# Key scores of the dilation-16 group moved out of the retention stage of a hybrid decoder step

## The chip, the cores and the metric

One core of a Trainium2 chip. The metric is the device time of one launch in microseconds (us), median of the runs. Before the change it is 1073.62 us over 3 runs (1072.58 to 1073.82).

## The reference

One step of a one-layer decoder for a prompt of 512 tokens and for 8 sample batches of 8 tokens, all in float32 (each product is made of three matmuls over high and low parts). A projection of x (1024 columns) to 10240 columns feeds two branches:

- A: attention with 4 head slots of 128 and three groups (window, dilation) = (128, 1), (512, 4), (2048, 16). A query reads the keys at distances 0, d, 2d, ..., window, with a penalty that grows with the distance. The sample queries read theirs from the caches of the 8 batches.
- B: retention with 4 heads (key 128, value 256), a carried state per batch, and a norm per head.

Both are gated, projected, merged, projected again and normalised. The caches are outputs too: every cache row from the eighth on is copied to the output, 8 rows further ahead, and the new keys and values are put behind.

For dilation 16 and cached keys, what concerns us is

```python
for b, q, h, m:   # 8 batches, 8 queries, 4 head slots, 128 keys
    s[b, q, h, m] = dot(query[b, q, h], cache2048[b, 16 * m + q, 0, h]) * scale - slope * (2048 - 16 * m)
```

Query q of a batch reads only the cache rows 16m + q: no two queries share a key.

## The kernel before

Instructions of five engines are written out by hand and tied by semaphores; every engine works through its own list in order. SyncE (SP) issues nearly all DMAs, on one queue. The stages:

**Attention stage** (span 24 to 409 us, a loop over 4 head slots of about 96 us). A head slot consumes six weight chunks of 1 MB. SP issues a chunk's two halves (`columns`, line 385) as soon as the half of `raw` is free, that is when its previous content has been split: ScalarE makes the high part (`high`, line 1132), VectorE the low part (`low`, line 1368) and increments `w_low`. Between chunks SP issues the copies of the caches of five batches (`rows`, line 417, DRAM to DRAM: 2.09 MB for each batch and head slot of the largest cache). TensorE projects in 27 units of about 3 us (`natural`, `transposed`) into two alternating banks, which VectorE empties (`unit_free`), and does the prompt's attention between the units. Unit 5 is the first of the second chunk, unit 10 the first of the third, unit 14 of the fourth, unit 18 of the fifth, unit 23 of the sixth. ScalarE's order (`attention_head`) ends with: `probs(1, 6)`, `next_high(5)` (the high part of the next head slot's first chunk), `sigmoid(23)`, `probs(2, 8)`, and so on; VectorE's `zr(0)` waits for `sigmoid(23)`, and TensorE's `output(1)` for VectorE's `output(0)` behind it. GpSimd stores keys and values (`store_kv`).

**Retention stage** (409 to 812 us, a loop over 4 retention heads of about 98 us, each with two sample batches x = 0, 1). For each batch SP loads 13 key tiles and then 13 value tiles of 128 x 512 (tile 0: dilation 1, tiles 1 to 4: dilation 4, tiles 5 to 12: dilation 16) into three slots (`load_tiles`, `keys`, `values`). A key tile is transposed by TensorE (4 transposes, line 680), split by ScalarE and VectorE (lines 1256 and 1574), and multiplied with block matrices of the queries (`score_tile`, 8 matmuls, line 919). `rows(x)` on VectorE collects the scores, then come softmax, the probabilities (`cached_probs`, `probs`) and the value tiles (`cached_output`, line 958). Units of the retention's own projections stand between. The low parts of the two weight chunks of the next head are made by GpSimd (lines 632 and 641). `vown`, 8 rows of 2 KB in each of three loads, are the batch's own values (line 479).

**Last stage** (812 to 1071 us): gates, branch projections, the copies of the caches of the other three batches, the output projection and the norm.

## Time and profile before

| | before |
|---|---|
| median of 3 runs | 1073.62 us |
| profiled execution: its own time, its span | 1073.26 us, 1071.40 us |
| TensorE matmul busy | 999.7 us (93%), mean granted clock 0.974 |
| VectorE, ScalarE, GpSimd busy | 539.9, 380.3, 151.2 us |
| DMA moved | 219.5 MB, mean 205 GB/s |
| attention stage, DMA share by halves of a head slot | 0.75 and 0.54 |
| retention stage from 440 us on, GB/s over stretches of 35 to 62 us | 153 to 211 |

The span is the time from the first to the last instruction on the core; the own time of the execution is 1.86 us longer. Busy times are summed over instructions, and matmuls overlap: a group's mean duration is longer than the time that the next one has to wait.

### The profile page before, as it was taken

The page shows a single profiled execution, that of the slowest core. Times are in us where ns is not written, and L with a number is a line of the kernel's source. Part 1 is how long each engine was busy: PE and PEld are TensorE (multiplying, and loading weights), DVE is VectorE, ACT ScalarE, POOL GpSimd, SP SyncE. Part 2 cuts the span into 40 slices and gives each one's busy share as a digit, 9 for nine tenths or more (in the row PEclk, how much of TensorE's full clock was granted, in tenths as well). Part 3 has the DMA queues.
Part 4 walks back from the last instruction along what each step waited for, and adds up shares of the span by engine and source line. Part 5 has one row for each costly group of instructions (what it writes and reads, how often), then busy time and mean ns, then how long its engine had stood idle before and what let it go on. Part 6 is the DMA issues. An engine that isn't in the chain of part 4 may idle for free.

```text
span 1071.4 us, 21575 instructions
## 1 busy us (share of the span) xinstructions
PE 999.7 (93%) x7796; PEld 926.7 (86%) x7796; DVE 539.9 (50%) x1017; ACT 380.3 (35%) x605; POOL 151.2 (14%) x149
## 2 busy tenths in 40 slices
PE   5999999999999999999989989999988999999892
PEld 5999999999999999778877777878757999999892
DVE  4246335433633454566656755675675433224338
ACT  4035213422431344345425442633454334333100
POOL 0001010101101012232312231322210000000003
PEclk8999999999999999999999999999988999999997
DMA  8775674767556564365638454643680888776602
GB/s 284 247 258 192 229 255 168 255 234 260 184 198 208 206 229 168 130 227 207 203 109 277 154 184 141 243 167 130 207 281 20 281 286 297 256 264 232 216 21 88
DMA packets 137317, 219.51 MB, mean 205 GB/s; under 512 B 7936, under 2 KB 102784, under 8 KB 135552
## 3 DMA queue, kind: packets, MB, share of 16 engines
q1 hardware_dynamic: 132704, 205.77, 56.5%
q0 software_dynamic: 3920, 10.89, 3.0%
q10 hardware_dynamic: 656, 2.36, 0.6%
q8 instruction: 23, 0.38, 0.2%
q14 instruction: 14, 0.11, 0.0%
HBM read 206.40 MB, written 99.88 MB: 286 GB/s over the span
## 4 chain that ended last, share of the span: by engine, by line
PE 84%; DVE 9%; ACT 3%; issue 2%; DMA 1%; DVEq 0%; ACTq 0%; SPq 0%; POOL 0%; POOLq 0%
PE bank L685 18%; PE bank L687 18%; PE bank L686 18%; PE bank L680 8%; PE bank L715 4%; PE bank L958 4%; PE bank L919 3%; DVE part_l L1574 3%; PE bank L772 2%; PE bank L794 2%; PE bank L994 1%; PE bank L1003 1%; PE bank L936 1%; ACT part_h L1256 1%; DMA xn<-in_x_prompt_dram 1%
## 5 line engine op out<-in xcount | busy, mean ns | idle before, releaser
L685 PE MATMUL bank<-xh,wh 128*128 128x288 f32 x640 | 193.1, 302 | 0.4 <-PE bank L1091 0.4
L685 PE MATMUL bank<-wh,xh 128*128 128x256 f32 x640 | 188.1, 294 | 3.5 <-DVE wl L1368 3.0
L687 PE MATMUL bank<-xh,wl 128*128 128x288 f32 x640 | 189.3, 296 | 0.0
L686 PE MATMUL bank<-xl,wh 128*128 128x288 f32 x640 | 189.2, 296 | 0.0
L686 PE MATMUL bank<-wl,xh 128*128 128x256 f32 x640 | 183.2, 286 | 0.0
L687 PE MATMUL bank<-wh,xl 128*128 128x256 f32 x640 | 183.1, 286 | 0.0
L685 PEld LDWEIGHTS bank<-wh,xh 128*128 128x128 f32 x640 | 125.3, 196 | 6.3 <-issue 3.4
L1132 ACT ACTIVATE wh<-raw 128x1024 fp32r<-128x1024 f32 (+1 forms) x104 | 101.2, 1018 | 80.1 <-PE bank L715 69.8
L686 PEld LDWEIGHTS bank<-wl,xh 128*128 128x128 f32 x640 | 125.2, 196 | 1.4
L687 PEld LDWEIGHTS bank<-wh,xl 128*128 128x128 f32 x640 | 124.8, 195 | 0.0
L685 PEld LDWEIGHTS bank<-xh,wh 128*128 128x128 f32 x640 | 121.0, 189 | 1.7 <-issue 1.4
L686 PEld LDWEIGHTS bank<-xl,wh 128*128 128x128 f32 x640 | 120.9, 189 | 1.0 <-issue 1.0
L1368 DVE TENSOR_TENSOR wl<-raw,wh 128x1024 fp32r<-128x1024 f32 (+1 forms) x90 | 102.3, 1173 | 36.8 <-ACT wh L1132 26.7
L687 PEld LDWEIGHTS bank<-xh,wl 128*128 128x128 f32 x640 | 120.8, 189 | 0.0
L1273 ACT ACTIVATE part_h<-cslot 128x512 fp32r<-128x512 f32 x104 | 59.4, 621 | 102.1 <-PE bank L958 101.6
L1574 DVE TENSOR_TENSOR part_l<-bank,part_h 128x512 fp32r<-128x512 f32 x104 | 71.1, 690 | 29.4 <-ACT part_h L1256 28.9
L1256 ACT ACTIVATE part_h<-bank 128x512 fp32r<-128x512 f32 x104 | 61.3, 597 | 49.7 <-PE bank L680 49.6
L1574 DVE TENSOR_TENSOR part_l<-cslot,part_h 128x512 fp32r<-128x512 f32 x104 | 66.6, 684 | 17.6 <-ACT part_h L1273 17.3
L919 PE MATMUL bank<-part_h,qm 128*64 128x128 f32 x416 | 68.5, 242 | 2.1 <-DVE part_l L1574 2.1
L577 POOL DMA_DIRECT2D out_dram<-kv x24 | 17.0, 710 | 353.0 <-DVE vn L1428 353.0
L680 PE MATMUL bank<-con,cslot 128*128 128x128 f32 x416 | 64.7, 281 | 2.0 <-DVE part_l L1574 1.5
L919 PE MATMUL bank<-part_l,qm 128*64 128x128 f32 x416 | 60.6, 222 | 0.0
(208 smaller groups left out, 1844.6 us busy)
## 6 DMA issues: line engine op xcount, KB each, us to landing
cslot<-in_cache_kv_w_dram SPq DMA_DIRECT2D x48, 1024.0 KB, 5.9
out_dram<-in_cache_kv_w_dram SPq DMA_DIRECT2D x20, 2040.0 KB, 10.4
raw<-in_w_in_dram SPq DMA_DIRECT2D x128, 256.0 KB
out_dram<-in_cache_kv_w_dram SPq DMA_DIRECT2D x24, 1020.0 KB, 9.5
out_dram<-in_cache_kv_w_dram SPq DMA_DIRECT2D x20, 504.0 KB, 5.2
raw<-in_w_in_dram SPq DMA_DIRECT2D x16, 512.0 KB
out_dram<-in_cache_kv_w_dram SPq DMA_DIRECT2D x24, 252.0 KB, 3.2
out_dram<-kv POOLq DMA_DIRECT2D x16, 256.0 KB, 3.3
```

What stands on the lines that cost most here:

```text
L680: return pe.transpose(out, in_, ident[0:k, 0:k])
L685: pe.matmul(out, lhs[0](k), rhs[0](k), start=(k == 0), stop=False)
L686: pe.matmul(out, lhs[0](k), rhs[1](k), start=False, stop=False)
L687: last = pe.matmul(out, lhs[1](k), rhs[0](k), start=False, stop=(k == n - 1))
L715: last = pe.matmul(out, pair[:, k, 0:P], part(k), start=(k == 0 and n == 0), stop=(k == KT_N - 1 and n == 1))
L919: last = pe.matmul(bank[4][0:BLK, g * P:(g + 1) * P], qm[:, o:o + BLK], part[j % 3][:, h * P:(h + 1) * P], start=(m == 0 and h == 0 and i ...
L958: last = pe.matmul(bank[4][0:BLK, :], probs, part[i % 3][0:n, :], start=(i == 0 and part is part_h), stop=(i == TILES and part is part_l))
L1132: act.activation(wh[par][:, s * HW:s * HW + n], wraw[s][:, 0:n], ACT.Copy).then_inc(w_high, 1)
L1256: act.activation(part_h[j % 3][:, :], bank[2 + j % 2][:, :], ACT.Copy).then_inc(part_high, 1)
L1273: act.activation(part_h[i % 3][:, :], cslot[s][:, k, :], ACT.Copy).then_inc(part_high, 1)
L1368: tt(wl[par][:, s * HW:s * HW + n], wraw[s][:, 0:n], wh[par][:, s * HW:s * HW + n].bitcast(F32), ALU.subtract).then_inc(w_low, 1)
L1574: tt(part_l[i % 3][:, :], src[:, :], part_h[i % 3][:, :].bitcast(F32), ALU.subtract)\
```

## The change

It has two parts.

1. The cached keys of dilation 16 (tiles 5 to 12 of the key tiles) are no longer loaded, transposed, split and multiplied in the retention stage; `KTILES` is 5. Instead, in each head slot h of the attention stage, SP loads these keys by query (`far_keys`): a partition holds one (half of m, batch, query), and 64 keys of 128 numbers, in three parts of 24, 24 and 16 keys into two buffers `far`. A part is 16 DMAs of 8 partitions each. GpSimd multiplies 8 keys at a time with the query's row (`qrow`; TensorE turns the queries `qdup`, ScalarE copies them out), and VectorE sums each product (`far_sum`, 8 per head slot, named among its other work). The sums go through DRAM (`fscr`) into `fars`, where `rows(x)` of the retention stage adds the penalty. `far_keys(h, 2)` waits for `far_sum(2)` of the same head slot and stands ahead of the sixth weight chunk; `far_keys(h, 0)` waits for the last sum of the head slot before.
2. The copies of the fifth batch's caches leave the attention stage and are issued in the retention stage, between that stage's loads. The low parts of the retention stage's weight chunks go from GpSimd to VectorE, at places of their own, and its order of units is changed: `value_unit(1)`, `value_unit(2)` and `cached_probs(0)` directly after `cached_scores(0)`, and the state groups inside `cached_output(0)`. Values of slots 1 and 2 of a head's first batch are loaded with the keys.

The core of the diff (semaphores, counts, and the reordering of ScalarE's and VectorE's lists that follows from it are left out):

```diff
-TILES = 13
+KTILES, TILES = 5, 13
 VTILES = TILES + 1
-PARTS = TILES + VTILES
+PARTS = KTILES + VTILES
...
+FAR = ((0, 24), (24, 48), (48, 64))
+FAR_PIECE = 8
+FAR_PIECES = 64 // FAR_PIECE
...
+            def far_keys(h, c):
+
+                lo, hi = FAR[c]
+                sp.wait_ge(far_summed, h * FAR_PIECES + (FAR_PIECES, 6, FAR_PIECES + 3)[c])
+                settle(sp)
+                src = caches[2].rearrange("b (m q) c h e -> b q m c (h e)", q=16)
+                for mh in range(2):
+                    for b in range(DEC_B):
+                        p = mh * 64 + b * DEC_T
+                        sp.dma_start(far[c % 2][p:p + DEC_T, 0:hi - lo, :],
+                                     src[b, 0:DEC_T, mh * 64 + lo:mh * 64 + hi, 0, bass.ds(h * DH, DH)])\
+                            .then_inc(far_in[c], 16)
...
                     columns(h * A_CH + (j + 1), (h * DH + a, h * DH + b), DH)
+                    if j < 2:
+                        far_keys(h, j)
                     rows(2, j, h * 510, 510)
                 columns(h * A_CH + 5, (h * RV + OFF_ZR,), CW)
-                rows(2, 4, h * 510, 510)
+                far_keys(h, 2)
...
-                for b in range(A_COPY_B):
+                for b in range(A_COPY_B - 1):
...
-                values(r * 2)
-                keys(r * 2 + 1, (0,))
+                values(r * 2, (0,))
+                keys(r * 2 + 1)
                 sp.wait_ge(states_out, r + 2)
                 if last:
                     gate_chunk(C0_C, 0)
                 else:
                     settle(sp)
                     retention_chunk(r * B_CH + (C0_B + 2), r + 1, 0)
-                keys(r * 2 + 1, (1, 2))
+                rows(2, A_COPY_B - 1, r * 510, 255)
+                values(r * 2 + 1)
                 if not last:
                     retention_chunk(r * B_CH + (C0_B + 3), r + 1, 1)
-                values(r * 2 + 1)
+                rows(2, A_COPY_B - 1, r * 510 + 255, 255)
+                rows(1, A_COPY_B - 1, r * 126, 126)
+                rows(0, A_COPY_B - 1, r * 30, 30)
                 if not last:
                     sp.wait_ge(rt_free[1], r * 9 + 6)
                     settle(sp)
                     head_constants(r + 1)
                     keys(r * 2 + 2)
+                    values(r * 2 + 2, (1, 2))
...
+                pool.wait_ge(far_row, h + 1)
+                for c, (lo, hi) in enumerate(FAR):
+                    pool.wait_ge(far_in[c], h * 256 + 256)
+                    for m in range(0, hi - lo, FAR_PIECE):
+                        a = far[c % 2][:, m:m + FAR_PIECE, :]
+                        tt(a, a, qrow[:, :].rearrange("p (a e) -> p a e", a=1).to_broadcast([P, FAR_PIECE, DH]),
+                           ALU.mult).then_inc(far_prod, 1)
                 pool.wait_ge(unit_free, h * A_UNITS + (3 + 23))
                 store_kv(h, 1)
+                pool.wait_ge(far_summed, h * FAR_PIECES + 2 * FAR_PIECES)
+                settle(pool)
+                pool.dma_start(fscr[bass.ds(h, 1), :, :].rearrange("h p m -> p (h m)"), fsum[:, :]).then_inc(far_out, 16)
+                pool.wait_ge(far_out, h * 16 + 16)
+                pool.sem_inc(far_free, 1)
...
+            for h in range(H):
+                pool.dma_start(fars[64 + h * DEC_T:64 + (h + 1) * DEC_T, :].rearrange("q (x m) -> q x m", m=64),
+                               fscr[h].rearrange("(x q) m -> q x m", q=DEC_T)).then_inc(far_back, 16)
...
-                for s in range(2):
-                    pool.wait_ge(w_high, r * (2 * B_CH) + (2 * C0_B + 4 + s + 1))
-                    tt(wl[0][:, s * HW:(s + 1) * HW], wraw[s], wh[0][:, s * HW:(s + 1) * HW].bitcast(F32),
-                       ALU.subtract).then_inc(w_low, 1)
...
+                    if u == 15:
+                        pe.wait_ge(unit_free, h * A_UNITS + (3 + 15))
+                        pe.wait_ge(o_read, h * QBLK + 1)
+                        turn(bank[2][:, P:2 * P], qdup[:, :]).then_inc(far_turned, 1)
...
+                act.wait_ge(far_summed, h * FAR_PIECES + FAR_PIECES)
+                act.wait_ge(far_turned, h + 1)
+                act.activation(qrow[:, :], bank[2][:, P:2 * P], ACT.Copy).then_inc(far_row, 1)
...
+                    dve.tensor_reduce(fsum[:, n * FAR_PIECE:(n + 1) * FAR_PIECE], far[c % 2][:, m:m + FAR_PIECE, :],
+                                      AX.X, ALU.add).then_inc(far_summed, 1)
...
                 values(18)
+                far_sum(0)
                 values(19)
                 low(c + 5, 1)
+                far_sum(1)
                 values(20)
                 softmax(2)
+                far_sum(2)
                 values(21)
                 probs(1, 5)
+                far_sum(3)
                 values(22)
                 softmax(3)
+                far_sum(4)
                 zr(0)
                 output(0)
                 probs(2, 7)
                 output(1)
+                far_sum(5)
                 low(c + 6, 0)
                 zr(1)
                 probs(3, 9)
+                far_sum(6)
                 output(2)
                 probs(3, 11)
                 zr(2)
+                far_sum(7)
                 output(3)
                 zr(3)
...
+                    o = fars[64:64 + ROWS, :].rearrange("p (a b m) -> p a b m", a=2, m=64)
+                    tt(srow[:, 2 * P:3 * P].rearrange("p (a m) -> p a m", a=2),
+                       o[:, :, bass.ds(r * 2 + x, 1), :].rearrange("p a b m -> p a (b m)"),
+                       const("biasc", ROWS)[:, 2 * P:3 * P].rearrange("p (a m) -> p a m", a=2), ALU.add)
...
-                lows(1, 0, 4, TILES)
+                lows(1, 0, 4, KTILES)
                 rows(1)
+                low(C0_C if last else r * B_CH + (C0_B + 2), 0)
                 normalise_rows(1)
...
-                lows(1, 1, 7, 11)
+                lows(1, 1, 7, 9)
+                if not last:
+                    low(r * B_CH + (C0_B + 3), 1)
+                lows(1, 1, 9, 11)
```

## Rows read from the trace of the kernel before

**Rows 1.** The profile's page: the chain that ended last, by engine

```profile
PE 84%; DVE 9%; ACT 3%; issue 2%; DMA 1%; DVEq 0%; ACTq 0%; SPq 0%; POOL 0%; POOLq 0%
```

**Rows 2.** A stretch: length, busy PE, PEld, DVE, ACT, POOL; clock, DMA share, GB/s

```profile
264.00:312.00 48.00, 47.66 (x366) 45.67 (x365) 23.98 (x45) 19.13 (x27) 3.88 (x6) 1.00 0.54 193
```

**Rows 3.** Timeline of TensorE and VectorE, second retention head: start, us, line

```profile
523.80 0.30 PE L919 MATMUL bank<-part_h,qm 128*64 128x128 f32 x1
...
536.53 1.56 PE L936 MATMUL bank<-ktn,qm 128*64 x24
...
578.19 1.28 DVE L1574 TENSOR_TENSOR part_l<-bank,part_h 128x512 fp32r<-128x512 f32 x2
...
586.53 0.69 DVE L1574 TENSOR_TENSOR part_l<-bank,part_h 128x512 fp32r<-128x512 f32 x1 [0.25 <-ACT part_h L1256]
```

**Rows 4.** Groups by line: score matmuls, and subtractions on VectorE and GpSimd

```profile
L1368 DVE TENSOR_TENSOR wl<-raw,wh 128x1024 fp32r<-128x1024 f32 (+1 forms) x90 | 102.3, 1173 | 36.8 <-ACT wh L1132 26.7 <-DMA lnb<-in_ln_b_dram 10.0
...
L919 PE MATMUL bank<-part_h,qm 128*64 128x128 f32 x416 | 68.5, 242 | 2.1 <-DVE part_l L1574 2.1
...
L632 POOL TENSOR_TENSOR wl<-raw,wh 128x1024 fp32r<-128x1024 f32 x8 | 18.9, 2375 | 61.3 <-ACT wh L1132 61.3
```

**Rows 5.** Timeline of VectorE, third attention head

```profile
231.53 0.43 DVE L1416 COPY kv<-bank 128x256 f32<-128x256 f32 x1
233.81 0.42 DVE L1416 COPY kv<-bank 128x256 f32<-128x256 f32 x1 [1.85 <-PE bank L687]
...
248.95 0.45 DVE L1403 TENSOR_SCALAR qt<-bank 128x288 f32<-128x288 f32 x1
...
283.04 1.22 DVE L1446 TENSOR_REDUCE nmax<-scoresp 128x1 f32<-128x1024 f32 x1
...
305.47 0.46 DVE L1408 TENSOR_TENSOR yb<-bank,sg 128x288 f32 x1 [3.24 <-ACT sg L1155]
```

**Rows 6.** Timeline of ScalarE, same head

```profile
286.81 2.00 ACT L1132 ACTIVATE wh<-raw 128x1024 fp32r<-128x1024 f32 x2 [1.01 <-PE bank L715]
288.83 1.28 ACT L1155 ACT_TABLE_LOAD   x1
292.13 0.41 ACT L1155 ACTIVATE sg<-bank 128x288 f32<-128x288 f32 x1 [2.01 <-PE bank L687]
```

**Rows 7.** Timeline of SyncE's DMA queue, same head

```profile
218.54 2.23 SPq L385 DMA_DIRECT2D raw<-in_w_in_dram  x4
...
258.56 1.54 SPq L385 DMA_DIRECT2D raw<-in_w_in_dram  x2
...
278.26 2.21 SPq L385 DMA_DIRECT2D raw<-in_w_in_dram  x4
```

**Rows 8.** DMA issues: a narrow load, and a wide one's landing

```profile
L479 SPq DMA_DIRECT2D vown<-out_dram x24: 277/294/578, 429.5 to 778.9; - x24
...
cslot<-in_cache_kv_w_dram SPq DMA_DIRECT2D x16, 256.0 KB, 2.9
```

**Rows 9.** Stretches: weight load, cache copy, loads of z (two), loads of vown

```profile
221.00:222.00 1.00, 1.00 (x11) 1.00 (x10) 0.00 (x0) 0.00 (x0) 0.00 (x0) 1.00 0.98 293
...
226.00:227.00 1.00, 1.00 (x10) 1.00 (x10) 0.42 (x1) 0.00 (x0) 0.00 (x0) 1.00 0.86 326
...
1000.00:1001.00 1.00, 1.00 (x6) 1.00 (x6) 0.00 (x0) 0.00 (x0) 0.00 (x0) 0.50 1.02 418
...
1002.00:1003.00 1.00, 1.00 (x11) 1.00 (x10) 0.00 (x0) 0.00 (x0) 0.00 (x0) 1.00 1.06 193
...
533.20:533.40 0.20, 0.20 (x5) 0.20 (x3) 0.20 (x1) 0.00 (x0) 0.00 (x0) 1.00 0.59 72
533.40:533.60 0.20, 0.20 (x6) 0.20 (x5) 0.20 (x1) 0.02 (x1) 0.00 (x0) 1.00 0.37 92
```

**Rows 10.** Stretches with the granted clock, end of the retention stage

```profile
812.00:814.00 2.00, 1.65 (x7) 1.56 (x8) 0.00 (x0) 1.50 (x1) 0.00 (x0) 0.50 0.00 0
...
816.00:818.00 2.00, 2.00 (x15) 2.00 (x14) 1.32 (x1) 2.00 (x1) 0.00 (x0) 0.82 0.00 0
```

More of the change, by code:

```diff
@@ L249, in bass_hybrid_step @@
         rinv = sb("rinv", [P, QBLK], F32, scope_a)
+        far = [sb(f"far{b}", [P, 24, DH], F32, scope_a) for b in range(2)]
+        qdup = sb("qdup", [P, P], F32, scope_a)
+        qrow = sb("qrow", [P, DH], F32, scope_a)
+        fsum = sb("fsum", [P, 64], F32, scope_a)
+        fscr = nc.dram_tensor("fscr", (H, P, 64), F32, kind="Internal").ap()
         scope_a.close()
@@ L473, in values @@
                     tiles = SLOTS[slot]
-                    load_tiles(b, 1, slot, tiles, PARTS + tiles[1])
+                    load_tiles(b, 1, slot, tiles, (PARTS if slot == 0 else KTILES) + tiles[1])
                     if slot == 0:
@@ L1712, in retention_head @@
                 values(0)
-                lows(0, 0, 2, TILES)
+                lows(0, 0, 2, KTILES)
+                rows(0)
+                values(1)
+                normalise_rows(0)
+                lows(0, 1, 0, 3)
+                values(2)
+                probs(0)
                 dve.wait_ge(hcon_in, r * 16 + 16)
@@ L1761, in retention_head @@
                 next_projected(2)
[L1762 removed]
+                lows(1, 1, 7, 9)
+                if not last:
+                    low(r * B_CH + (C0_B + 3), 1)
+                lows(1, 1, 9, 11)
                 normalise()
```

143 lines of the change are left out of this document (70 added, 73 removed).

## The prediction

> **What bounds the kernel now.** I read the chain of waits first: 84% of it is TensorE [rows 1]. Then the stretches: in the second half of a head slot of the attention stage TensorE is busy 47.66 of 48 us, VectorE half of that time, GpSimd 3.88 us [rows 2]. So nearly every microsecond of TensorE work taken away shortens the kernel, and every stall of TensorE lengthens it. The DMA share of 0.54 there looks like room. But a share is a mean; what counts is which load stands ahead of the one that TensorE needs next.
>
> **What the change takes away.** The score matmuls are listed with 242 ns each [rows 4], and 8 of them for each of 64 key tiles would be 124 us. That is wrong, as they overlap. The timeline gives the real price: in the second retention head the 13 key tiles of x = 0 run from 523.80 to 536.53 [rows 3], 0.98 us each, so 8 tiles are 7.8 us. In x = 1 VectorE splits tiles 4 and 5 from 578.19 on and tile 12 until 587.2 [rows 3]; tiles 5 to 12 are 8.3 us. Together 16.1 us a head, 64 us in all.
>
> **What the retention stage gives back.** GpSimd's two pairs of subtractions, 2.375 us a piece, go to VectorE, which needs 1.17 us for one [rows 4]. In x = 1 the first pair now stands after `rows(1)`: TensorE has about 2.9 us of output groups to do after the last score, VectorE 2.3 us of `rows` and 2.4 us of lows, so the next projection starts some 1.8 us late. The second pair falls into the value tiles, where VectorE has little spare time: 1.2 us. I take 3 us for three heads and 1.5 us for the last, 10 us; the bounds are 0 and 17 (all of VectorE's new time on the path). For x = 0 I followed the new order through: the probabilities come out under units 1 and 2, and the stalls are as long as before. Its DMAs sum to about 16 MB a head, against 18 MB now, and come between waits that leave them time; the copies of the fifth batch cost nothing here as long as the values of x = 1 (3.4 MB, issued when its fifth key tile is split) land within the some 16 us until TensorE's sixth value tile. **Retention: -54 us.** At the hand-over GpSimd's four small DMAs and their landing stand ahead of `a_end` and of VectorE's first work: +2 us.
>
> **What the attention stage pays.** GpSimd's 8 products (up to 2.4 us each, as its subtractions of the same size, rows 4) and VectorE's 8 sums (1.22 us each, as the maximum over 1024 numbers, rows 5) a head slot lie beside TensorE work; both engines are idle half the time or more. 2 us in all for what sticks out, with the 4 turns. The price is in the loads.
>
> *The wait in SP's queue.* Now SP issues the sixth chunk's successor at 278.26 [rows 7], and ScalarE takes it at 286.81, then loads a table and does `sigmoid(23)` at 292.13 [rows 6]; VectorE's `zr(0)` and `output(0)` follow within 2 us and release TensorE. With the change `far_keys(h, 2)` stands ahead of it and waits for `far_sum(2)`, after the reduction of 283.04: 284.26 + 1.22 = 285.5. SP has stood there since the two DMAs at 258.56 [rows 7]. Then come 16 narrow issues: 0.294 us each for one of 8 partitions [rows 8], with address work about 0.5 us, 8.0 us in all. Queued behind this wait are four weight DMAs and eight copies; behind the weights wait ScalarE's whole list, VectorE's `zr(0)`, TensorE's `output(1)`. The stall can't be less than that of the issues alone.
>
> *How fast narrow loads run* the trace shows only in part. A weight load moves 293 GB/s, a cache copy 326 [rows 9]. The load of `z` goes at 418 GB/s over 128 partitions and at 193 over 64, at the same DMA share [rows 9]: the rate goes with the partitions. The three 8-partition loads of `vown` pass in slices of 72 and 92 GB/s [rows 9]. So the bounds are 82 (their mean) and 293 GB/s. I take 130: above the nearest row, as its 48 KB hold a start and an end, and a train of 16 can overlap. The Trainium skill (DMA: Bandwidth & Descriptors, "How many engines (k)") says that a DMA uses as many engines as divide the slowest dimension of both sides, 8 here, which would be half of 293, or 147 GB/s, and a result of 1089 us by the working below.
>
> *The sum for a head slot, at 130 GB/s.* Parts 0 and 1 are 1.57 MB (12.1 us), part 2 is 1.05 MB (8.1 us). A wide 256 KB load lands 2.9 us after its issue [rows 8], of which 0.9 is transfer: 2.0 us on top of a queue's transfers.
> - Part 2: 285.5 + 8.1 + 3.6 (the weights at 293 GB/s) + 2.0 = 299.2; ScalarE's second half 1.0, the table 1.3: `sigmoid(23)` at 301.5 instead of 292.13, **9.4 us**. TensorE's granted clock is 0.50 in the 4 us after it starts again at 812, and 0.82 in the next 2 [rows 10]: full speed comes back about 5 us late, **2 us** more.
> - Part 0 is issued when the last sum is done, after the product at 305.47: 307.1, or 211.1 on the clock of the head slot shown (96 us earlier). Its 12.1 us, the copy behind it (2.09 MB, 6.4 us) and the weights (3.6 + 2.0) end at 235.2; ScalarE and VectorE need 2.2 us for them and 0.4 for the copy of unit 5, now at 231.53, which may end at 233.8, where the next unit's copy starts [rows 5]: 237.8, **4.0 us**. Now these weights, issued at 218.54 [rows 7], find an empty queue.
> - Part 1 goes out behind them, from 234.5: 12.1 + 6.4 + 3.6 + 0.7 + 2.6 = 259.9, where VectorE's 248.95 [rows 5] may slip to 252, now 256: **3.9 us**.
>
> 19.3 us a head slot, 77 us in all. Moving the fifth batch's copy away helps none of the three, since it stood behind the fifth chunk.
>
> **Sum,** against the profiled execution's own 1073.26 (0.4 under the median): -54 + 2 + 2 + 77 = +27, **1100 us**.
>
> **The rivals.**
> - *Narrow loads run as wide ones.* At 293 GB/s parts 0 and 1 are out of the way in time and only the wait of part 2 stays, by its issues: 11.5 us a head slot with the clock, 46 us: 1069 us; with nothing given back in the retention stage 1059. For it speaks that no narrow train is in the trace; against it the row of 193 GB/s. It decides from about 12 us lost a head slot: below, the change is faster. Chance 0.24.
> - *Narrow loads run at 82 GB/s.* Part 0 takes 19.2 us, part 2 12.8 us. Stalls: 14.1 + 2, 11.1 and 11.0 us, 38 us a head slot: 1176 us. For it speak the rows of `vown`; against it that a load may overtake the stuck one. Chance 0.17. The Trainium skill (SBUF — State Buffer, "Door 1: The DMA port swizzle") gives each 4 neighbouring partitions one port of about 27 GB/s, so 8 partitions 54 GB/s, which would make about 1280 us; the rows of 193 and 72 GB/s go its way.
> - *VectorE becomes the bound in the retention stage* (17 us given back instead of 10): 1107 us, the same side; it only widens.
>
> **How the numbers follow.** The forecast's case has 0.53, the first rival 0.24, the second 0.17; 0.06 is for an outcome near the old time. The forecast's case spans 1080 (147 GB/s and less given back) to 1130 (105 GB/s). The range of 1055 to 1150 adds the first rival whole; it leaves out most of the second. 0.2% (2.1 us) is about what a measurement tells from no change: faster 0.25, same 0.05, slower 0.70.
>
> **What the profile after would show.** Right: score matmuls 160 instead of 416 of each kind; retention heads of about 84 us instead of 98; in each head slot a TensorE gap of about 9 us before `output(1)` that ends with ScalarE behind a DMA of weights, and gaps of 3 to 5 us at units 7 and 13; head slots of 115 us instead of 96; a DMA share near half during the narrow loads. Wrong: weights that land in time behind parts 0 and 1, or a gap at `output(1)` under 7 us (issues under 0.4 us); a gap over 12 us would be the slow rival; retention heads over 88 us would say that VectorE or the values' loads bind there.

## The result and the profile after

The changed kernel takes 1176.95 us (median of 4 runs, 1172.77 to 1196.41) beside 1073.72 us for the kernel before on the same chip: ratio 1.094, 95% interval 1.090 to 1.099. Ratios, here and below, leave out the executions that took over 1.5% longer than the fastest of the same kernel, here the one of 1196.41 us. The forecast was 1100 us with a range to 1150; the prediction had the side right and the size wrong, by 77 us. The second rival had named 1176 us.

The profiled execution took 1172.77 us (span 1171.1). First the chain of waits, by engine; before, TensorE had 84% of it and SP's queue nothing [rows 1]:

```profile
PE 54%; SPq 15%; issue 8%; DVE 8%; DMA 8%; POOL 3%; ACT 2%; DVEq 0%; POOLq 0%; ACTq 0%
```

Of the chain, 23% now belong to SP's queue and to DMAs; the question is in which stage. Two instructions mark the stages: VectorE's low half of the sample queries, the first thing it does after the attention stage, and the last of the eight `pn` matmuls, near the end of the retention stage. A row gives count, shortest/median/longest ns, and the first and last start. Before:

```profile
L1529 DVE TENSOR_TENSOR qhl<-qhl x1: 959/959/959, 412.0 to 412.0; 128x768 fp32r<-128x768 f32 x1
L958 PE MATMUL bank<-part_h,pn x8: 443/446/681, 472.6 to 806.5; 24*64 24x512 f32 x8
```

After:

```profile
L1583 DVE TENSOR_TENSOR qhl<-qhl x1: 959/959/959, 580.1 to 580.1; 128x768 fp32r<-128x768 f32 x1
L999 PE MATMUL bank<-part_h,pn x8: 443/447/681, 629.8 to 906.4; 24*64 24x512 f32 x8
```

So the attention stage is 168 us longer (580.1 - 412.0). From there to the end of the span it was 659.4 us and is 591.0: **68 us shorter**, of which 57 lie between the first and the last `pn` matmul (333.9 and 276.6 us). 168 - 68 = 100 us, the difference of the spans. From marker to end, a stretch (columns as in [rows 2]) and waits of TensorE that changed (total, times, longest), before:

```profile
412.00:1071.40 659.40, 601.23 (x4721) 538.26 (x4719) 359.72 (x689) 252.99 (x440) 118.17 (x93) 0.96 0.57 194
PE bank L958 <- DVE part_l L1574: 13.3, 17, 3.2
PE bank L680 <- DVE qdt L1730: 8.4, 4, 2.1
```

After:

```profile
580.10:1171.10 591.00, 536.31 (x3948) 476.93 (x3947) 332.12 (x647) 209.66 (x349) 84.14 (x79) 0.96 0.60 207
PE bank L999 <- DVE part_l L1628: 9.3, 12, 3.2
PE bank L722 <- DVE wl L1399: 5.1, 4, 1.5
```

So 65 of the 68 us are TensorE work that is gone (601.23 - 536.31), and 3.5 are idle time that is gone. The score matmuls are 160 of each kind instead of 416 [rows 4]:

```profile
L960 PE MATMUL bank<-part_h,qm 128*64 128x128 f32 x160 | 25.5, 241 | 4.8 <-DVE part_l L1628 4.8
...
L621 POOL TENSOR_TENSOR far<-far,qrow 128x1024 f32<-128x1024 f32 x32 | 75.3, 2382 | 190.9 <-DMA far<-in_cache_kv_w_dram 113.4 <-ACT qrow L1226 77.5
...
L1532 DVE TENSOR_REDUCE fsum<-far 128x8 f32<-128x1024 f32 x32 | 38.7, 1210 | 0.9 <-DVE yb L1443 0.9
```

The new work costs what its nearest rows said (2.38 and 1.21 us each); but GpSimd stood 113 us in front of its loads, over the four head slots.

Where the attention stage lost its time shows in one head slot, 246 to 386 us. What TensorE waited for there (total, times, longest):

```profile
PE bank L834 <- DVE on L1495: 18.7, 1, 18.7
PE bank L722 <- DVE kv L1451: 16.7, 1, 16.7
PE bank L722 <- DVE qt L1438: 7.7, 1, 7.7
```

Three gaps, 43 us, in the three places that the prediction had named: `output(1)`, unit 7, unit 13. The first two come in all four head slots (13 to 19.5 us each); the third, at unit 13, is 7.7 us here, 2.3 us in the slot before, and missing in the first and the last. The same slot in stretches (columns as in [rows 2]), and three stretches inside narrow trains (a train is the row of transfers that makes up one part):

```profile
256.00:266.00 10.00, 0.52 (x5) 0.28 (x3) 0.39 (x1) 0.00 (x0) 0.00 (x0) 0.72 1.01 94
266.00:276.00 10.00, 0.79 (x3) 0.79 (x4) 1.64 (x5) 5.99 (x7) 7.72 (x7) 0.50 1.08 306
...
316.00:326.00 10.00, 0.00 (x0) 0.00 (x0) 0.00 (x0) 0.08 (x1) 0.00 (x0) 0.62 0.83 208
326.00:336.00 10.00, 5.19 (x26) 5.19 (x27) 3.21 (x4) 2.03 (x2) 0.00 (x0) 0.52 0.64 92
...
252.00:254.00 2.00, 2.00 (x17) 2.00 (x16) 1.97 (x4) 0.00 (x0) 0.00 (x0) 1.00 0.65 67
302.00:304.00 2.00, 2.00 (x19) 2.00 (x19) 0.41 (x1) 0.00 (x0) 0.00 (x0) 1.00 0.65 59
338.00:340.00 2.00, 2.00 (x19) 2.00 (x18) 0.42 (x1) 0.00 (x0) 0.00 (x0) 1.00 0.65 88
```

During part 2 (252 to 254) the queue moves 67 GB/s, during part 0 (302 to 304) 59, and 88 in part 1, where 130 had been assumed; a weight load moves 293 [rows 9]. The DMA share of 0.65 does not warn of it: the engines show as busy while they move little. The granted clock is 0.50 to 0.72 over the stretches with the gaps, so a gap costs a little more than its length. SP's queue in the same slot (start, us):

```profile
221.33 1.56 SPq L396 DMA_DIRECT2D raw<-in_w_in_dram  x2
248.55 8.45 SPq L440 DMA_DIRECT2D far<-in_cache_kv_w_dram  x16
257.36 7.46 SPq L396 DMA_DIRECT2D raw<-in_w_in_dram  x4
265.11 8.29 SPq L428 DMA_DIRECT2D out_dram<-in_cache_kv_w_dram  x8
281.12 2.23 SPq L396 DMA_DIRECT2D raw<-in_w_in_dram  x4
```

SP stands from 222.9 to 248.55 before it can issue part 2, and four weight DMAs come behind it at 257.36. These are the first chunk of the next head slot. The sixth chunk is the pair at 221.33: what the section on the change says of part 2, that it stands ahead of the sixth chunk, is one chunk off. It stands behind the sixth and ahead of the next head slot's first, as the prediction's working has it ("the sixth chunk's successor").

### The profile page after: what moved, and what is told of

The parts are those of the page before. It is cut to its first block, busy times and chain, and to the rows that moved or that the text cites. A ratio compares the mean times of both kernels' runs of the same rounds, so it can differ in the third digit from the quotient of the medians.

```text
span 1171.1 us, 20225 instructions
## 1 busy us (share of the span) xinstructions
PE 958.4 (82%) x7032; PEld 887.2 (76%) x7032; DVE 548.4 (47%) x1011; ACT 340.2 (29%) x518; POOL 197.0 (17%) x175
## 4 chain that ended last, share of the span: by engine, by line
PE 54%; SPq 15%; issue 8%; DVE 8%; DMA 8%; POOL 3%; ACT 2%; DVEq 0%; POOLq 0%; ACTq 0%
PE bank L722 13%; PE bank L723 12%; PE bank L724 12%; SPq L440 10%; DMA raw<-in_w_in_dram 7%; SPq L396 5%; PE bank L999 4%; PE bank L717 3%; PE bank L752 2%; PE bank L834 2%; DVE part_l L1628 1%; PE bank L1044 1%; PE bank L809 1%; PE bank L1035 1%; DMA xn<-in_x_prompt_dram 1%
## 5 line engine op out<-in xcount | busy, mean ns | idle before, releaser
L722 PE MATMUL bank<-wh,xh 128*128 128x256 f32 x640 | 192.5, 301 | 67.9 <-DVE kv L1451 59.2
L722 PE MATMUL bank<-xh,wh 128*128 128x288 f32 x640 | 197.6, 309 | 10.4 <-DVE qt L1438 10.0
L723 PE MATMUL bank<-wl,xh 128*128 128x256 f32 x640 | 187.3, 293 | 0.0
L1399 DVE TENSOR_TENSOR wl<-raw,wh 128x1024 fp32r<-128x1024 f32 (+1 forms) x104 | 120.0, 1184 | 121.9 <-ACT wh L1173 107.7
L722 PEld LDWEIGHTS bank<-xh,wh 128*128 128x128 f32 x640 | 124.8, 195 | 12.1 <-DVE qt L1438 10.5
L724 PEld LDWEIGHTS bank<-wh,xl 128*128 128x128 f32 x640 | 129.2, 202 | 0.0
L621 POOL TENSOR_TENSOR far<-far,qrow 128x1024 f32<-128x1024 f32 x32 | 75.3, 2382 | 190.9 <-DMA far<-in_cache_kv_w_dram 113.4
L834 PE MATMUL bank<-kv,pt 128*128 128x128 f32 x216 | 32.4, 310 | 75.2 <-DVE on L1495 75.2
L834 PEld LDWEIGHTS bank<-kv,pt 128*128 128x128 f32 x216 | 30.4, 222 | 76.2 <-DVE on L1495 76.2
L1862 DVE TENSOR_TENSOR uc<-bank,sgc 128x288 f32<-128x288 f32 x32 | 14.6, 457 | 92.7 <-PE bank L724 92.7
L1443 DVE TENSOR_TENSOR yb<-bank,sg 128x288 f32 x16 | 7.3, 457 | 98.6 <-ACT sg L1196 98.6
```

Source lines behind the costliest of these rows:

```text
L621: tt(a, a, qrow[:, :].rearrange("p (a e) -> p a e", a=1).to_broadcast([P, FAR_PIECE, DH]), ALU.mult).then_inc(far_prod, 1)
L722: pe.matmul(out, lhs[0](k), rhs[0](k), start=(k == 0), stop=False)
L723: pe.matmul(out, lhs[0](k), rhs[1](k), start=False, stop=False)
L724: last = pe.matmul(out, lhs[1](k), rhs[0](k), start=False, stop=(k == n - 1))
L834: last = pe.matmul(bank[2][:, 0:P], pt[:, bi % 2, x * P:(x + 1) * P], kv[:, k, (G + g) * DH:(G + g + 1) * DH], start=(x == 0), stop=(x == ...
L1399: tt(wl[par][:, s * HW:s * HW + n], wraw[s][:, 0:n], wh[par][:, s * HW:s * HW + n].bitcast(F32), ALU.subtract).then_inc(w_low, 1)
```

## The experiments

Every time below is the median of its own runs; the kernel before had medians of 1073.7 to 1075.6 us beside them. "Marker" is the start of the instruction on `qhl` shown above, in the profiled execution: the end of the attention stage. A profiled execution can lie off the median: mostly by less than 5 us, in two kernels by 7, but the first series with the copies first was profiled at 1191.8 us, the second at 1143.8, and the strided kernel from GpSimd's queue, issued later, at 1077.8.

| kernel | us | marker, us |
|---|---|---|
| before / after | 1073.7 / 1177.0 | 412.0 / 580.1 |
| 16 neighbouring partitions | 1101.7 | 506.5 |
| 8 partitions, 4 apart | 1138.6 | 544.6 |
| 16 partitions, 8 apart ("strided") | 1063.2 | 468.2 |
| strided, third part last | 1026.8 | 431.8 |
| narrow, third part last | 1074.9 | 476.6 |
| narrow, only SP's wait in the old place | 1125.1 | 531.8 |
| strided, only SP's wait in the old place | 1039.6 | 448.7 |
| no dilation-16 work at all | 1005.2 | 413.8 |
| strided last, thin products and sums | 1016.3 | 425.0 |
| strided last, fifth batch back | 1029.3 | 439.6 |
| strided last, parts 0 and 1 a chunk later | 1027.5 | 436.4 |
| strided last, copies first | 1025.2 | 434.7 |
| narrow, copies first, two series | 1158.2, 1153.7 | 599.2, 551.2 |
| narrow / strided from GpSimd's queue | 1147.9 / 1065.4 | 557.0 / 479.9 |
| the same, issued later | 1085.9 / 1068.2 | 489.6 / 485.9 |

**1. Is it the rate, and what sets it?** The kernel issues each part as 16 transfers, one for each batch and half, of 8 neighbouring partitions (the 8 query positions). Three other ways to move the same 512-byte pieces to the same buffers:

```
# e_neighbours: one transfer for each query position q, rows in the order (q, batch, half)
-   sp.dma_start(far[c % 2][p:p + DEC_T, 0:hi - lo, :], src[b, 0:DEC_T, ...])      # 16 times
+   sp.dma_start(far[c % 2][q * 16:q * 16 + 16, 0:hi - lo, :], src[:, q, lo:hi, ...])  # 8 times
# e_strided: rows in the order (batch, half, q)
+   sp.dma_start(far[c % 2][q:q + 15 * DEC_T + 1:DEC_T, 0:hi - lo, :], src[:, q, lo:hi, ...])
# e_spread: 16 transfers, p = j // 4 * 32 + j % 4
+   sp.dma_start(far[c % 2][p:p + 4 * DEC_T - 3:4, 0:hi - lo, :], src[j // 2, 0:DEC_T, ...])
```

The first two reorder the queries and the sums to fit.

> The same bytes to the same buffers, but a part comes as 8 transfers of 16 neighbouring partitions (one query position q each) in place of 16 transfers of 8 neighbouring ones. Theory P (what limits the narrow loads is how many write ports of SBUF their few neighbouring partitions reach; partitions that lie far apart would go faster): 16 neighbours reach at most twice as many as 8, so the part runs at 60 to 120 GB/s instead of the 59 to 67 measured, and the time falls only partly, to 1080 to 1177 us. Theory E (a transfer of 8 partitions occupies only 8 of the 16 DMA engines, and where the partitions lie does not matter): 16 partitions occupy all 16 engines, so the rate is that of the strided layout of the next run, and the two times are the same. Theory S (the read side in DRAM, 512-byte pieces 64 KB apart, sets the rate): no change, 1170 to 1180 us.

> As the run before (8 transfers of 16 partitions, the same DRAM pieces in each), but the 16 partitions lie 8 apart and so are spread over the whole of SBUF. Theory P: the rate rises towards that of the wide loads (200 to 293 GB/s), and the time is 1030 to 1060 us, well under the run with 16 neighbours. Theory E: the same time as with 16 neighbours, whichever it is. Theory S: 1170 to 1180 us as the changed kernel.

> Still 16 transfers of 8 partitions a part, but the 8 partitions lie 4 apart instead of side by side. The query columns are not reordered, so the dilation-16 scores are of wrong queries; the work and its times are the same. Theory P: 8 partitions 4 apart reach four times the ports of 8 side by side; the rate doubles at least, to 120 GB/s or more, and the time is 1050 to 1120 us. Theory E: 8 engines at the same rate each, no change, 1170 to 1180 us. Theory S: no change either.

Measured: 1101.7 us (ratio to before 1.022, interval 1.018 to 1.027), 1063.2 (0.988, 0.985 to 0.991), 1138.6 (1.060, 1.055 to 1.064). Stretches inside the trains, first 16 neighbours, then 16 strided, then 8 spread:

```profile
230.00:232.00 2.00, 2.00 (x18) 2.00 (x17) 1.97 (x2) 0.00 (x0) 0.00 (x0) 1.00 1.24 118
268.00:270.00 2.00, 1.32 (x11) 1.12 (x10) 1.86 (x4) 0.00 (x0) 0.00 (x0) 1.00 1.28 112
```

```profile
214.00:216.00 2.00, 2.00 (x18) 2.00 (x17) 1.97 (x3) 0.00 (x0) 0.00 (x0) 1.00 0.56 148
250.00:252.00 2.00, 2.00 (x19) 2.00 (x18) 1.60 (x3) 0.00 (x0) 0.00 (x0) 1.00 1.21 188
```

```profile
290.00:292.00 2.00, 2.00 (x19) 2.00 (x19) 1.30 (x3) 1.73 (x2) 0.00 (x0) 1.00 0.40 110
292.00:294.00 2.00, 2.00 (x19) 2.00 (x18) 1.50 (x3) 0.00 (x0) 0.00 (x0) 1.00 0.41 123
```

The read side is the same in all, so DRAM is not what limits (theory S falls). Neighbours against strided: same number of transfers, same partitions in each, same pieces, only the distance differs, and 38 us come off; theory E alone falls, P stands. 8 neighbours against 8 spread, at a higher price to issue (0.70 us each instead of 0.43): 38 us again. The share points the same way: in these rows neighbours move 59 GB/s at a share of 0.65 or 118 at 1.24, some 90 to 95 per unit of engine time; spread moves 110 at 0.40, 275 per unit, up to three times as much. It is no fixed price of a layout: strided moves 264 per unit in the first of its rows and 155 in the second, and the last heading shows narrow trains of 154 GB/s at a share of 0.61. But P is not all: doubling the neighbours from 8 to 16 doubled the rate, and the spread train is held by its issues (16 in 14.4 us, 98 KB each, 109 GB/s). The Trainium skill (SBUF — State Buffer, "Door 1: The DMA port swizzle") gives every 4 neighbouring partitions one port of about 27 GB/s, with 32 partitions apart on the same port again. By that rule 8 neighbours get 54, 16 neighbours 108, and 16 partitions 8 apart only 8 ports, 216 GB/s; the rows have 59, 112 to 118, and 148 to 188. The trace agrees with its order and nearly with its sizes here; the narrow trains of a higher rate under the last heading, 104 to 154 GB/s with 8 neighbours, lie far above its 54.

**2. Where the third part stands.** `far_keys(h, 2)` is moved behind the weights that stood behind it, the next head slot's first chunk (in the last head slot the retention stage's first). The expectations call this "behind the sixth chunk's columns", one chunk off:

```
     columns(h * A_CH + 5, (h * RV + OFF_ZR,), CW)
-    far_keys(h, 2)
     if last: ... else: columns(h * A_CH + 6, ...)
+    far_keys(h, 2)
```

> The strided loads, and the third part of a head's dilation-16 keys is issued behind the sixth chunk's columns instead of ahead of them (in the last head it stays ahead of the retention stage's first columns, since both branches of the issue list put it right behind or ahead). Theory P with order: the wait of SP for the second part's sums no longer holds back the weights of the next head, so a further 3 to 7 us per head for three heads come off against the strided run: 1012 to 1040 us, under the kernel before. If the order does not matter: within 3 us of the strided run.

> The changed kernel with its narrow loads, the third part of a head's keys issued behind the sixth chunk's columns, in all four heads. Theory R (the rate of the narrow loads is the loss, since all three parts of 26, 26 and 17 us pass through one queue ahead of weights): some of the wait only moves to the next head's second chunk, so 5 to 30 us come off, 1145 to 1172 us. Theory O (the loss is mostly SP's wait for the second part's sums with weights queued behind it): the same 36 us come off as between the two strided runs, or more, so 1141 us or less.

(The first of these expectations is unsure of the last head; in both kernels the third part is last in all four.) Measured: strided 1026.8 us (ratio 0.955, 0.952 to 0.959), **under the kernel before**; narrow 1074.9 (0.997, 0.993 to 1.001; single runs from 1061 to 1086). Theory O wins clearly for the narrow loads: one line moved takes 102 us off, against 36 with the strided ones. That moved SP's wait for the sums together with the transfers. Then only the transfers were moved, and SP's wait for the sums left where it was:

```
-    far_keys(h, 2)
+    sp.wait_ge(far_summed, h * FAR_PIECES + (FAR_PIECES + 3))
     if last: ... else: columns(h * A_CH + 6, ...)
+    far_keys(h, 2)
```

> The changed kernel with only the transfers of the third part behind the sixth chunk's columns; SP's wait for this head's first three sums stays ahead of them. Moving wait and transfers together took 102 us off (1177 to 1075). Theory W (it is the wait: the sixth chunk's columns cannot be issued until VectorE has made its third sum, which itself waits for the late first part): most of the 102 us is back, 1140 to 1177 us. Theory T (it is the 17 us that the narrow transfers themselves take ahead of the columns): within 15 us of 1075 us.

> The same with the strided loads, between 1063 us (wait and transfers ahead) and 1027 us (both behind). Theory W: 1050 to 1063 us. Theory T: 1027 to 1037 us.

Measured: 1125.1 us (interval of the ratio 1.036 to 1.049) and 1039.6 (0.964 to 0.970). Neither theory has it alone: with narrow loads the transfers out of the way take 52 us off and the wait moved too another 50; with strided ones 24 and 13. What TensorE waited for, over the whole kernel, in the changed one:

```profile
PE bank L834 <- DVE on L1495: 75.2, 4, 19.5
PE bank L722 <- DVE kv L1451: 59.2, 5, 16.7
```

with the wait alone in the old place:

```profile
PE bank L724 <- DVE kv L1453: 57.7, 5, 16.8
PE bank L724 <- DVE qt L1440: 21.7, 3, 10.8
PE bank L836 <- DVE on L1497: 12.7, 4, 3.7
```

and with both moved:

```profile
PE bank L722 <- DVE kv L1451: 28.4, 7, 12.2
PE bank L834 <- DVE on L1495: 10.4, 8, 2.3
```

The transfers ahead of the weights made the gap at `output(1)` (75 us down to 13; the waits for `qt` rose from 10 to 22). The gap at unit 7 (`kv`) stayed until the wait moved too. But then the same transfers also ran faster, as told under the last heading. Part 0 of the third head slot, with the wait in the old place:

```profile
272.00:274.00 2.00, 2.00 (x19) 2.00 (x18) 1.21 (x3) 1.91 (x3) 0.00 (x0) 1.00 0.65 77
```

and with both moved:

```profile
252.00:254.00 2.00, 2.00 (x19) 2.00 (x18) 0.00 (x0) 0.05 (x1) 0.00 (x0) 1.00 0.62 111
```

So the 50 us hold two things, the wait and a faster part 0, and how they share them is not shown; the strided pair has 13 us for its wait.

**3. The rest of the change alone.** All dilation-16 work is left out (those cached scores are then zero before the bias), with the waits for it on TensorE and ScalarE; the retention stage and the copies stay as changed.

```
-    far_keys(h, j) ... far_keys(h, 2)                     # SP, all three parts
-    tt(a, a, qrow...)  ...  far_sum(0) ... far_sum(7)     # products and sums
-    turn(bank[2][:, P:2 * P], qdup[:, :]) ... act.activation(qrow[:, :], ...)
-    pool.dma_start(fscr...) ... pool.dma_start(fars[...], fscr[h]...)
+    pool.memset(fars[64:64 + ROWS, :], 0.0).then_inc(far_back, 16 * H)
```

> The changed kernel without the dilation-16 loads, products, sums and the detour of the queries: the dilation-16 scores of the cached keys are left out (zero before the bias), everything else of the change stays, the fifth batch's copies in the retention stage too. Theory of the prediction: the retention part of the change is worth 54 us net, so 1015 to 1022 us. Theory from the changed kernel's trace (the give-back of 10 us by the low halves on VectorE did not come): the time from the end of the attention stage on is 66 us shorter, so 1005 to 1012 us. Rival: the retention heads are short only because the late attention stage left the copies less to contend with; then over 1025 us.

Measured: 1005.2 us (ratio 0.933, 0.928 to 0.938), with the marker and a stretch:

```profile
L1544 DVE TENSOR_TENSOR qhl<-qhl x1: 957/957/957, 413.8 to 413.8; 128x768 fp32r<-128x768 f32 x1
```

```profile
100.00:200.00 100.00, 99.33 (x778) 96.87 (x777) 46.12 (x85) 30.53 (x41) 9.62 (x15) 1.00 0.58 194
```

The attention stage is as long as before (413.8 against 412.0): with TensorE busy 99.33 of 100 us, moving the fifth batch's copies out has nothing to gain there. The whole 69 us are the retention stage's, as in the changed kernel; the rival, that they come from a late attention stage, falls. That leaves a floor: a version with free dilation-16 work would take 1005 us, and the strided one with the third part last pays 22 us over it.

**4. What those 22 us are.** Products and sums on 8 of 128 elements, the scores then of 8 elements only:

```
-    a = far[c % 2][:, m:m + FAR_PIECE, :]
+    a = far[c % 2][:, m:m + FAR_PIECE, 0:8]     # and the same in qrow and in the sum
```

> The strided version with the third part last, but products and sums work on 8 of the 128 elements only (the dilation-16 scores are of 8 elements): all loads, waits and instruction counts stay, 19 us of GpSimd and 10 us of VectorE a head go to about a quarter. Theory L (what is left of the loss against the version without the dilation-16 work is loads in the queue ahead of weights): within 5 us of the 1026.8 us measured with whole products. Theory V (it is VectorE's sums that delay the low halves and evictions in order behind them): 8 us or more come off, 1008 to 1018 us.

Measured: 1016.3 us. 10.5 us are engine time of products and sums (theory V); the other 11 are the loads with what the thin products and sums still take, not taken apart. Over 200 to 300 us TensorE is busy 98.69 of 100, against 96.61 with whole ones. How much of the 10.5 is VectorE's and how much GpSimd's was not tried. The fifth batch's copies put back into the attention stage:

```
     columns(h * A_CH + 5, (h * RV + OFF_ZR,), CW)
+    rows(2, 4, h * 510, 510)
-    for b in range(A_COPY_B - 1):
+    for b in range(A_COPY_B):
...
-    rows(2, A_COPY_B - 1, ...) ... rows(0, A_COPY_B - 1, ...)     # stage_b
```

> The strided version with the third part last, and the fifth batch's copies (20 MB of traffic read and written) back in the attention stage as before the change. Theory Q (moving them made room in the attention stage's queue, which the new loads need): 10 to 25 us slower than 1026.8 us. Rival (they fit in either stage): within 3 us. Second rival: the retention stage gains more than the attention stage loses, 1015 to 1023 us.

Measured: 1029.3 us (1028.0 to 1031.8), against 1026.8 (1024.7 to 1031.2): the marker is 7.8 us later and what follows is 2.2 us shorter in the profiled executions, and the medians differ by 2.5 us, within the rival's 3. Moving the copies does next to nothing. Parts 0 and 1 a chunk later in the queue:

```
-    if j < 2:
-        far_keys(h, j)
+    if j in (1, 2):
+        far_keys(h, j - 1)
```

> The strided version with the third part last (1026.8 us), and the first and second part each one chunk later in SP's queue (behind the second and third chunk's columns). If only the third part's wait and place mattered: within 3 us. If each part costs by the chunk that stands behind it: the first head gains about 4 us at its start, where TensorE was idle for 4.2 of 36 us (24 to 60 us) that the version without dilation-16 work keeps busy, the others nothing: 1020 to 1026 us. If the products then come late for the sums: over 1030 us.

Measured: 1027.5 us (1019.7 to 1033.3), within the 3 us of the first expectation. The first head gains at its start and gives it back at once; stretches with parts 0 and 1 early, then late:

```profile
24.00:60.00 36.00, 31.80 (x240) 31.60 (x240) 8.76 (x18) 3.18 (x3) 1.58 (x3) 0.90 1.12 295
60.00:100.00 40.00, 40.00 (x306) 39.02 (x305) 22.32 (x38) 13.22 (x19) 16.53 (x10) 1.00 0.53 174
```

```profile
24.00:60.00 36.00, 36.00 (x290) 36.00 (x289) 12.66 (x23) 5.55 (x6) 3.93 (x6) 0.98 1.04 282
60.00:100.00 40.00, 36.24 (x257) 35.03 (x256) 18.25 (x32) 10.95 (x16) 14.09 (x6) 0.91 0.54 179
```

**5. The same loads from another queue.** `far_keys` is called by GpSimd instead of SP, so that no weight stands behind a narrow transfer in a queue.

```
 with pool.Fori(0, H) as h:
+    far_keys(h, 0)                                  # pool.dma_start in it
+    far_keys(h, 1)
     pool.wait_ge(unit_free, h * A_UNITS + (3 + 10))
...
                ALU.mult).then_inc(far_prod, 1)
+            if c == 1 and m == 0:
+                far_keys(h, 2)
```

> The changed kernel's narrow loads, the same transfers, but issued from GpSimd's queue (the first two parts of a head at the start of its turn, the third after the first product of the second part), so that no weight stands behind them in a queue. Theory Q (what costs is that weights stand behind slow transfers in one queue): 1015 to 1045 us, whatever the rate of the narrow loads. Theory B (narrow loads take the DMA engines' time itself, so weights are late from any queue): 1060 us or more. A third cost would be GpSimd's own time to issue 48 transfers a head.

> The same with the strided loads, 24 transfers a head from GpSimd's queue. Theory Q: about 10 to 15 us under the strided version with the third part last, 1010 to 1020 us, near the 1016 us of thin products; the rest to the 1005 us without dilation-16 work is VectorE's sums. Theory B: 1027 us or more, as there.

Measured: 1147.9 and 1065.4 us, on theory B's side. Both were clouded: the first parts ran against the kernel's first loads (TensorE waited 28.7 and 27.2 us for its first input `xn`, 10 us in the kernels of experiment 2), and GpSimd itself waited 13.8 us before it could issue the third part of the first head. A second pair takes both away (the first two parts at unit 10, the third behind the last product of the second part):

```
-    far_keys(h, 0)
-    far_keys(h, 1)
     pool.wait_ge(unit_free, h * A_UNITS + (3 + 10))
+    far_keys(h, 0)
+    far_keys(h, 1)
...
-            if c == 1 and m == 0:
+            if c == 1 and m == 16:
```

> Narrow loads from GpSimd's queue as before, but a head's first two parts are issued when its unit 10 is read (not at the start of its turn, so not against the kernel's first weights), and the third behind the last product of the second part (GpSimd no longer holds products back for it). Theory Q (weights behind slow transfers in one queue are the loss): under 1075 us, the narrow loads' best from SP's queue, and near 1040. Theory B (the narrow loads take the engines' time from the weights in any queue): 1100 to 1148 us, as the first run from this queue.

> The same with the strided loads. Theory Q: 1010 to 1027 us. Theory B, with strided loads at half the engine time for a byte: 1030 to 1065 us, and the step from narrow to strided is 50 us or more, as it was from SP's queue.

Measured: 1085.9 us (1.005 to 1.012 of before) and 1068.2. The narrow version gains 91 us over the changed kernel but stays above the best one from SP's queue, far from the 1040 of theory Q; the strided one is 41 us worse than from SP's queue, and the step from narrow to strided is 18 us where theory B wanted 50. So neither theory holds as stated. In the strided one's profile, of its longest execution, TensorE stops while and after the parts (issued from 279.7 to 290.2), the weights (from 284.4) and a 2 MB cache copy (from 286.9) are in flight together:

```profile
290.00:300.00 10.00, 8.63 (x65) 8.16 (x64) 2.04 (x3) 1.66 (x2) 4.06 (x7) 1.00 1.10 213
300.00:310.00 10.00, 1.14 (x5) 1.14 (x6) 2.22 (x5) 1.67 (x3) 0.11 (x1) 0.59 1.02 325
```

Here a second queue did not hide a transfer from the one that TensorE needs next. That they share the engines, and that SP's order had at least let the urgent weights go first, is my reading and not shown; only two times of issue were tried, and how much a better one could win stays open.

## Why the prediction was wrong

- **Side and mechanism: right.** The change loses in the attention stage more than it wins in the retention stage, through narrow loads ahead of weights in SP's queue.
- **The step that failed: "I take 130"** for the rate of the narrow loads, "above the nearest row, as its 48 KB hold a start and an end, and a train of 16 can overlap". It measured 59 to 67 GB/s in parts 0 and 2 and 88 in part 1 of the slot shown. With the prediction's own working and these rates, part 0 takes 26 us instead of 12.1, part 1 17.8, part 2 16: gaps of 18 (4.0 + 14), 9.6 (3.9 + 5.7) and 17 us (9.4 + 8). Measured: 16.7, 7.7 and 18.7. So the model of the queue was sound, and a factor of two in the rate of parts 0 and 2 made the attention stage 168 us longer where some 80 had been forecast; a retention gain 14 us above the forecast hid part of that, which leaves 77 in the median. Part 1 of the second and fourth slots ran at 115 and 125 to 156 GB/s, not far from the 130, and the gap at unit 13 was 2.3 us and none there. The lower bound of 82 GB/s, the mean of the two `vown` slices [rows 9], was itself too high: parts 0 and 2, trains of 16 transfers, ran no faster than the three short `vown` loads. The rival at 82 GB/s came to 1176 us with two gaps too small (14.1 and 11.1), one too large (11.0) and a retention gain that is too small; that it met the median is partly luck.
- The rule of the Trainium skill (SBUF — State Buffer, "Door 1: The DMA port swizzle") was on record beside that rival, at 54 GB/s, and was given no weight of its own. Its rate was the nearest to the 59 to 67 GB/s of parts 0 and 2. The 1280 us worked out from it did not come: part 1 ran at 88 to 156.
- **Retention, -54 us: too small.** Measured -68 (-69 without the dilation-16 work); heads of 82 us (the `pn` casts of x = 0 start at 607.0, 689.2, 770.8 and 852.3) where 84 were forecast. The 64 us for the tiles were right: 65 us of TensorE work are gone. What failed is the net give-back of 10 us: the idle time fell by 3.5 us instead. The give-back itself is there, TensorE waits 5.1 us for low halves (`wl`), 0.3 before. But the forecast that all other stalls stay as long as before was wrong: the 8.4 us for `qdt` are gone and the waits for `part_l` in the value tiles fell by 4.0 us, against 6 us that other waits rose. The change reorders VectorE's list as well; which step of it took these waits away was not tried.
- **Compute, +2:** the 10.5 us of experiment 4 are the price of products and sums where TensorE is busy. "2 us in all for what sticks out" is too little there; in the changed kernel the gaps may hide part of it, which was not tried. **Hand-over, +2:** VectorE waits 4.0 us for `fars` ahead of the marker, TensorE only 1.2 us for the first copy `qk` behind it (0.6 before): about right.
- **"Moving the fifth batch's copy away helps none of the three":** right, by experiments 3 and 4.
- **Head slots of 115 us:** they were about 140. Matmul counts, the places of the gaps and their releasers came as forecast, the third gap in two slots only.
- The rival "narrow loads run as wide ones", 1069 us, is what the strided version does (1063.2), by other loads: 16 partitions, 8 apart, instead of 8 neighbours.

**What the experiments leave as the best version:** strided transfers with the third part behind the next head slot's first chunk, 1026.8 us, 4.5% under the kernel before and 12.8% under the changed one; with the copies ahead of the first two parts it is the same (1025.2, below).

## What to carry to other kernels

Before a load is laid out so that its partitions suit the arithmetic, count how many partitions one transfer touches and how far apart they lie: here the same bytes in the same pieces took the DMA engines up to three times the time in the trains of the low rate, and a reordering of (batch, half, query), so that a transfer has 16 partitions 8 apart instead of 8 side by side, was worth 114 us. A transfer whose issue waits for compute belongs behind everything in its queue that does not; here one line moved was worth 36 us with strided loads and 102 with narrow ones, which ran faster with it. And where a sum hangs on one rate that no row shows, the range should follow that rate over its whole uncertainty, below the lowest row too.

## What the hardware showed that was not expected

The same train of narrow transfers has two rates. In the changed kernel, part 1 of the fourth head (472 to 474) moves 154 GB/s where part 0 of the third (302 to 304, above) moves 59, at nearly the same share (0.61 and 0.65):

```profile
472.00:474.00 2.00, 0.00 (x0) 0.00 (x0) 1.23 (x2) 1.06 (x1) 0.00 (x0) 0.50 0.61 154
```

In the narrow kernel with the third part last, parts 0 and 1 of the second and third head run mostly at 104 to 151, part 0 of the fourth at 101 to 112 in its second half, and part 2 at 64 to 73. Here part 1 of the third head:

```profile
270.00:272.00 2.00, 2.00 (x19) 2.00 (x19) 1.23 (x1) 0.65 (x2) 0.00 (x0) 1.00 0.63 104
276.00:278.00 2.00, 2.00 (x11) 2.00 (x11) 0.00 (x0) 0.00 (x0) 0.00 (x0) 0.50 0.62 132
```

Most trains at the low rate had started with nothing else in flight, and most at the high rate behind weights still in flight. Not all: with only SP's wait in the old place, part 1 of the second head is issued from 164.75 on, with weights in flight, and runs at 68:

```profile
163.00:165.00 2.00, 0.00 (x0) 0.00 (x0) 0.00 (x0) 0.00 (x0) 0.00 (x0) 0.50 0.73 300
176.00:178.00 2.00, 2.00 (x11) 2.00 (x11) 0.00 (x0) 0.00 (x0) 0.00 (x0) 0.50 0.65 68
```

An exchange was to decide: the 2 MB copy that follows each of the first two parts goes ahead of it.

```
+    rows(2, j, h * 510, 510)
     if j < 2:
         far_keys(h, j)
-    rows(2, j, h * 510, 510)
```

> The changed kernel with one thing exchanged: the cache copy (2 MB) that follows each of a head's first two narrow parts is issued ahead of it. The bytes ahead of the next weights stay the same. Theory D (a narrow train that starts while another transfer is in flight runs at 110 to 155 GB/s, one that starts into an empty queue at 60 to 74): part 0 now runs at 110 GB/s or more in every head, 1.57 MB take 12 to 14 us instead of 24 to 26, and 8 to 12 us a head come off: 1130 to 1150 us. Theory N (the rate depends on which rows and partitions the part touches, not on what is in flight): part 0 stays at 60 to 74 GB/s and the time within 10 us of 1177 us.

> The strided version with the third part last (1026.8 us) and the same exchange. Theory D: the strided loads run at 190 to 230 GB/s either way, the same bytes stand ahead of the weights, so within 4 us of 1026.8 us, and under it if the first products do not come late. If the parts then come too late for GpSimd: 1030 us or more.

Measured: 1158.2 us with single runs from 1137.6 to 1191.8 (ratio 1.061, 1.058 to 1.065), and 1025.2 for the strided one, as expected. The narrow one's profile was of its longest execution. A second series of it:

> The same kernel as with the copies first. Theory D (trains that start behind a transfer in flight are fast): its undisturbed time is 1135 to 1150 us, and in a profile of such an execution parts 1 of heads two to four, which start behind the copy in flight, run at 100 GB/s or more, where they ran at 64 in the profile of the 1192 us execution. Theory X (the rate of a train is drawn anew in each execution, whatever is in flight): times spread over 1135 to 1195 with no two values, and slow and fast trains are mixed in the profile.

Measured: 1153.7 us, single runs 1142.9, 1143.8, 1153.3, 1154.0, 1173.1 and 1203.3 (ratio 1.070, 1.065 to 1.074); profile of the 1143.8 us execution. In it a part 0 (second head) that started with little in flight, then a part 1 (third head) with a copy in flight at its start:

```profile
166.00:168.00 2.00, 2.00 (x19) 2.00 (x18) 2.00 (x2) 0.81 (x1) 0.00 (x0) 1.00 0.62 141
305.00:308.00 3.00, 0.33 (x3) 0.12 (x2) 0.00 (x0) 0.98 (x1) 0.00 (x0) 1.00 1.43 495
314.00:316.00 2.00, 2.00 (x11) 2.00 (x11) 0.00 (x0) 0.00 (x0) 0.00 (x0) 0.50 0.66 79
```

The first runs at the high rate, the second, with 495 GB/s in flight at its start, at the low one: the reverse of theory D. Theory X holds better: trains of both rates are mixed, and so are the times, which have no two values. The ratios of 1.061 and 1.070, against 1.094 for the changed kernel, say that the exchange did win 2 to 3%, about where theory D had put the time, but not by D's mechanism; what won it is not shown. Why 8 neighbouring partitions are served at twice the rate in some trains stays open; whether in those several transfers, to different partitions, were in flight at once was not looked at. What can be said: over its two series this narrow kernel spread by 66 us, the two narrow ones of experiment 2 by 25, the strided ones of experiments 1 and 2 by 3 to 7, the other strided ones by up to 14.
